# A fused hybrid decoder layer on one core: x turned unscaled as it lands, the first norm's factor spread over partitions by a product with ones

## The reference, cut to what matters

```python
xn = x * rsqrt(mean(x * x, axis=-1) + 1e-6) * g_mix      # 256 tokens, 2048 features
proj = xn @ w_in                                          # w_in: 2048 x 6144
xx = token_shift(xn) - xn
x_w, x_a, x_g = (xn + xx * mu_x[j] for j in range(3))     # inputs of three small products
# differential attention on the first 3072 columns of proj, RWKV-7 on the last 3072,
# output projection, second RMSNorm, top-2 of 32 SwiGLU experts, final RMSNorm
```

## Time and profile before

| what | value |
|---|---|
| median of 3 runs | 1580.76 us (1580.16 to 1580.87) |
| span of the profiled execution, first to last instruction | 1578.8 us (its own time is shown as this span alone) |
| PE busy | 1338.9 us, 85% |
| DVE busy | 454.4 us, 29% |
| ACT busy | 323.8 us, 21% |
| POOL busy | 44.0 us, 3% |
| moved by DMA | 481.06 MB, 305 GB/s on the mean |

### The profile page before, as it was taken

How to read it: one execution, slowest core, us unless ns; L and a number is a source line. 1 busy time by engine, 2 the same in 40 slices (tenths; PEclk the granted TensorE clock), 3 DMA queues, 4 the chain that set the end, 5 groups by cost and what they waited for, 6 DMA issues and landing times.

```text
span 1578.8 us, 22501 instructions
## 1 busy us (share of the span) xinstructions
PE 1338.9 (85%) x9378; PEld 722.1 (46%) x9378; DVE 454.4 (29%) x1100; ACT 323.8 (21%) x760; POOL 44.0 (3%) x95
## 2 busy tenths in 40 slices
PE   7999999999999999987776886876876877867776
PEld 6888888888886545422222222222221222222223
DVE  6032646767644641401101101101101101111103
ACT  1013112344422421211111111111111111111112
POOL 3000000001110000000000000000000000000000
PEclk9999999999999999998989888888888888897988
DMA  9433322222334267599999999999999999999996
GB/s 306 162 107 107 107 81 82 81 82 83 108 110 158 87 237 322 204 433 433 429 434 430 433 430 433 430 433 431 433 432 432 432 432 432 432 433 431 433 430 265
DMA packets 62055, 481.06 MB, mean 305 GB/s; under 512 B 8565, under 2 KB 27654, under 8 KB 48934
## 3 DMA queue, kind: packets, MB, share of 16 engines
q1 hardware_dynamic: 61106, 478.89, 74.3%
q10 hardware_dynamic: 884, 1.23, 0.2%
HBM read 478.01 MB, written 2.10 MB: 304 GB/s over the span
## 4 chain that ended last, share of the span: by engine, by line
PE 56%; DMA 41%; DVE 1%; ACT 1%; issue 1%; DVEq 0%; SPq 0%; ACTq 0%
DMA ring<-in_moe_w_gate_dram 22%; DMA ring<-in_moe_w_up_dram 17%; PE ps L960 11%; PE ps L773 9%; PE ps L1203 8%; PE ps L1045 7%; PE ps L1222 3%; PE ps L1179 3%; DMA ring<-in_moe_w_down_dram 2%; PE ps L846 2%; PE ps L989 2%; PE ps L1230 2%; PE ps L834 1%; PE ps L1214 1%; PE ps L852 0%
## 5 line engine op out<-in xcount | busy, mean ns | idle before, releaser
L1203 PE MATMUL ps<-ring,oT 128*32 128x512 f32 x2048 | 333.5, 811 | 205.3 <-DMA ring<-in_moe_w_gate_dram 115.2
L1203 PEld LDWEIGHTS ps<-ring,oT 128*32 128x32 f32 x2048 | 82.6, 142 | 452.1 <-issue 310.6
L960 PE MATMUL ps<-xT,ring 128*128 128x256 f32 x768 | 185.1, 388 | 0.0
L2136 DVE TENSOR_TENSOR oT<-oT,ps 128x128 f32<-128x128 f32 x32 | 9.2, 287 | 582.8 <-ACT oT L1587 582.8
L960 PEld LDWEIGHTS ps<-xT,ring 128*128 128x128 f32 x768 | 140.3, 190 | 20.6
L773 PE MATMUL ps<-xT,ring 128*128 128x256 f32 x640 | 139.5, 380 | 0.0
L773 PEld LDWEIGHTS ps<-xT,ring 128*128 128x128 f32 x640 | 121.2, 190 | 17.8 <-issue 1.5
L1222 PE MATMUL ps<-ring,oT 128*32 128x512 f32 x1024 | 117.9, 600 | 8.7 <-DVE oT L2136 7.8
L1179 PE MATMUL ps<-xT,oT 128*32 128x512 f32 x512 | 115.3, 1030 | 0.4 <-DVE oT L2124 0.4
L1045 PE MATMUL ps<-ring,oT 128*128 128x512 f32 x256 | 113.3, 594 | 0.8 <-ACT oT L1539 0.8
L1214 PEld LDWEIGHTS ps<-fold,oT 128*128 128x128 f32 x512 | 59.6, 192 | 39.7 <-issue 39.7
(11 more groups left out here) (336 smaller groups left out, 1247.1 us busy)
## 6 DMA issues: line engine op xcount, KB each, us to landing
ring<-in_moe_w_gate_dram SPq DMA_DIRECT2D x32, 4096.0 KB, 32.5
ring<-in_moe_w_up_dram SPq DMA_DIRECT2D x31, 4096.0 KB, 33.2
ring<-in_moe_w_down_dram SPq DMA_DIRECT2D x31, 4096.0 KB, 32.5
ring<-in_w_in_dram SPq DMA_DIRECT2D x24, 1024.0 KB, 5.2
ring<-in_w_in_dram SPq DMA_DIRECT2D x32, 768.0 KB, 4.8
ring<-in_w_out_dram SPq DMA_DIRECT2D x16, 1024.0 KB, 5.5
ring<-in_moe_w_up_dram SPq DMA_DIRECT2D x2, 2048.0 KB, 10.9
ring<-in_moe_w_down_dram SPq DMA_DIRECT2D x2, 2048.0 KB, 30.8
```

Of the source, the lines that this page charges most:

```text
L960: last = mm(ps[:, 6 + (par + c) % 2, 0:S], wv[:, k, c * P:(c + 1) * P], xT[:, kq * KQ + k, :], start=(kq == 0 and k == 0), stop=(kq == 3 a ...
L1203: last = mm(ps[c * B:(c + 1) * B, 1 + j, :], xe[:, par, k, :], w[:, k, :], start=(kq == 0), stop=(kq == 3), tile_position=(0, c * B))
```

## The change

The tile `xn` goes. PE turns x itself, each token half as soon as it has landed (`s_x`). The factor takes another way: DVE multiplies the identity by it (`scales`, a diagonal matrix of 128 tokens for each token half); PE multiplies a matrix of ones by that, which puts the factor of token j into column j of every partition; DVE copies these 256 columns out of the right half of PSUM's bank 7 (`spread`). `xT` is then made by one operation a block, turned block x g_mix (per partition) x `spread` (per column), and DVE does all 16 (before, DVE and ACT did 8 each). The copy of the turned rows to `vec` goes from DVE to ACT, ahead of its four lambda loads. Blocks 14 and 15 are turned after `spread` has been copied (`s_vec` 2), since block 15 goes to where the product lay. Two small operations of DVE (`omka`, `subg`) move behind the 16. ACT's semaphore `s_xTa` goes; PE waits for `s_xT` with doubled counts.

```diff
--- before.py
+++ after.py
@@ -260,7 +260,6 @@
         s_xn = sem("xn_ready")
         s_xt = sem("xn_turned")
         s_xT = sem("xT_ready")
-        s_xTa = sem("xT_ready_by_scalar")
         s_pr = sem("rkv_block_projected")
         s_prA = sem("rkv_block_copied")
         s_mix = sem("lora_input_mixed")
@@ -479,7 +478,8 @@
         SOLVES = ((0, 1), (2,), (3, 4), (5, 6), (7,), (8,), (9,), (10,), (11,))
         DENSE = (4, 2, 2, 3, 2, 3, 2, 3, 3)
         HALVES = (4, 6, 7, 9, 10, 12, 13, 14)
-        xn = oT.rearrange("p k s -> p (k s)").rearrange("p (t d) -> p t d", t=TT)
+        scales = oT[:, 0, :].rearrange("p (t q) -> p t q", t=TT)
+        spread = oT[:, 1, :]
 
         def load_rows(eng, dst, group):
 
@@ -722,23 +722,26 @@
 
             def turn(k, t):
                 return pe.transpose(ps[:, k // 2, (k % 2) * S + t * P:(k % 2) * S + (t + 1) * P],
-                                    xn[:, t, k * P:(k + 1) * P], ident[:, :])
-
+                                    res[:, t, k * P:(k + 1) * P], ident[:, :])
+
+            pe.wait_ge(s_x[0], 16)
             for k in range(KT - 2):
-                if k % 8 == 0:
-                    pe.wait_ge(s_xn, k // 8 + 1)
                 turn(k, 0)
             pe.wait_ge(s_rows, 16 * ROW_LOADS)
             pe.transpose(vec_ps[:, 0:NA_ROWS], rows_a[0:NA_ROWS, :], ident[0:NA_ROWS, 0:NA_ROWS])
             pe.transpose(vec_ps[:, NA_ROWS:NA_ROWS + NB_ROWS], rows_b[0:NB_ROWS, :],
                          ident[0:NB_ROWS, 0:NB_ROWS]).then_inc(s_vecT, 1)
+            pe.wait_ge(s_x[1], 16)
             for k in range(KT - 2):
-                if k % 8 == 0:
-                    pe.wait_ge(s_xn, k // 8 + 3)
                 last = turn(k, 1)
                 if k % 2:
                     last.then_inc(s_xt, 1)
             pe.wait_ge(s_vec, 1)
+            for t in range(TT):
+                pe.wait_ge(s_xn, t + 1)
+                last = mm(ps[:, 7, S + t * P:S + (t + 1) * P], ones[:, :], scales[:, t, :], start=True, stop=True)
+            last.then_inc(s_vecT, 1)
+            pe.wait_ge(s_vec, 2)
             for k in (KT - 2, KT - 1):
                 for t in range(TT):
                     last = turn(k, t)
@@ -756,17 +759,14 @@
 
             def rkv_block(n, fold=False, outs=False):
                 for kq in range(4):
-                    pe.wait_ge(s_xT, 2 * kq + 2)
-                    pe.wait_ge(s_xTa, 2 * kq + 2)
+                    pe.wait_ge(s_xT, 4 * kq + 4)
                     pe.wait_ge(s_ring[kq], n * 16 + 16)
                     wv = eslot[kq].rearrange("p (k n) -> p k n", k=KQ)
                     for c in range(4):
                         if kq == 0:
                             pe.wait_ge(s_prA, n * 4 + c + 1)
-                        if kq == 0 and c == 2:
-                            pe.wait_ge(s_xT, 4)
-                        if kq == 0 and c == 3:
-                            pe.wait_ge(s_xTa, 4)
+                        if kq == 0 and c >= 2:
+                            pe.wait_ge(s_xT, 2 * c + 2)
                         if kq == 0 and outs:
                             pe.wait_ge(s_l3, 2 * MT + MT // 2 + c + 1)
                         for k in range(KQ):
@@ -1324,17 +1324,14 @@
                 act.wait_ge(s_hsq, t + 1)
                 a.activation(rs[:, t:t + 1], ss[:, t:t + 1], ACT.Sqrt, bias=ssv[:, TT + t:TT + t + 1],
                              scale=1.0 / D).then_inc(s_std, 1)
+            act.wait_ge(s_vecT, 1)
+            a.copy(vec[:, 0:NA_ROWS + NB_ROWS], vec_ps).then_inc(s_vec, 1)
             act.dma_start(lamrow[:, 0, :], da_lambda_q1.broadcast_to([P, 64])).then_inc(s_lam, 16)
             act.dma_start(lamrow[:, 1, :], da_lambda_k1.broadcast_to([P, 64])).then_inc(s_lam, 16)
             act.dma_start(lamrow[:, 2, :], da_lambda_q2.broadcast_to([P, 64])).then_inc(s_lam, 16)
             act.dma_start(lamrow[:, 3, :], da_lambda_k2.broadcast_to([P, 64])).then_inc(s_lam, 16)
 
             act.wait_ge(s_vec, 1)
-            for b in (1, 3, 5, 7):
-                act.wait_ge(s_xt, b + 1)
-                for k in (2 * b, 2 * b + 1):
-                    a.activation(xT[:, k, :], ps[:, b, (k % 2) * S:(k % 2 + 1) * S], ACT.Copy,
-                                 scale=col(V_GMIX + k)).then_inc(s_xTa, 1)
             def rkv_copies(n):
                 for c in range(4):
                     if c < 3:
@@ -1653,23 +1650,23 @@
                 v.tensor_scalar(ssv[:, TT + t:TT + t + 1], ssv[:, t:t + 1], 1.0 / D, 1e-6, ALU.mult, ALU.add).then_inc(s_hsq, 1)
                 dve.wait_ge(s_std, t + 1)
                 own.mark(v.reciprocal(rs2[:, t:t + 1], rs[:, t:t + 1]))
-                own.join()
-                for half in (slice(0, D // 2), slice(D // 2, D)):
-                    v.tensor_scalar(xn[:, t, half], res[:, t, half], rs2[:, t:t + 1], None, ALU.mult).then_inc(s_xn, 1)
-            dve.wait_ge(s_vecT, 1)
-            v.tensor_copy(vec[:, 0:NA_ROWS + NB_ROWS], vec_ps).then_inc(s_vec, 1)
-            dve.wait_ge(s_vec, 1)
+                if t == 0:
+                    dve.wait_ge(s_mask, 3)
+                own.join()
+                v.tensor_scalar(scales[:, t, :], ident[:, :], rs2[:, t:t + 1], None, ALU.mult).then_inc(s_xn, 1)
+            dve.wait_ge(s_vecT, 2)
+            v.tensor_copy(spread, ps[:, 7, S:2 * S]).then_inc(s_vec, 1)
+            dve.wait_ge(s_vec, 2)
+            for k in range(KT):
+                if k % 2 == 0:
+                    dve.wait_ge(s_xt, k // 2 + 1)
+                v.scalar_tensor_tensor(xT[:, k, :], ps[:, k // 2, (k % 2) * S:(k % 2 + 1) * S], col(V_GMIX + k), spread,
+                                       ALU.mult, ALU.mult).then_inc(s_xT, 1)
+
             dve.wait_ge(s_mask, 4)
             own.mark(v.tensor_scalar(omka, col(V_KA, MT), -1.0, 1.0, ALU.mult, ALU.add))
             own.mark(v.tensor_scalar(subg, col(V_SUB), 1.0 - LAM0, None, ALU.mult))
-            for b in (0, 2, 4, 6):
-                dve.wait_ge(s_xt, b + 1)
-                for k in (2 * b, 2 * b + 1):
-                    v.tensor_scalar(xT[:, k, :], ps[:, b, (k % 2) * S:(k % 2 + 1) * S], col(V_GMIX + k), None,
-                                    ALU.mult).then_inc(s_xT, 1)
-
-            dve.wait_ge(s_xT, 8)
-            dve.wait_ge(s_xTa, 8)
+            dve.wait_ge(s_xT, KT)
             own.mark(v.tensor_tensor(diff[:, :, 1:S], xT[:, :, 0:S - 1], xT[:, :, 1:S], ALU.subtract))
             own.mark(v.tensor_scalar(diff[:, :, 0:1], xT[:, :, 0:1], -1.0, None, ALU.mult))
             own.join()
```

## The result

The changed kernel takes 1583.18 us (median of 20 runs, 1580.50 to 1585.03), the kernel before 1580.64 us beside it (20 runs, 1579.69 to 1581.67). The ratio is 1.0014, 95% interval [1.0008, 1.0021], so the change costs 1.3 to 3.3 us. That is within 0.2% by its middle, and a loss. The scatter has grown too, from 2.0 to 4.5 us.

The account below looks back on a forecast made before the run. PE was taken as the bound, with nothing covering the head before the first projection matmul. Rows, second turns, product, copy and VectorE's blocks moved its start from 15.62 to 17.03: 1580.76 + 1.4 = 1582.2 us, range 1579.7 to 1584.8.

Parts of the forecast that it names:

- The whole effect is the shift of the first projection matmul: Head: nothing covers what precedes this matmul, so its start's move from 15.62 to 17.03, +1.4 us, passes to the end.
- the sign that the whole is wrong: At the end: the end moves by another amount than the first projection matmul does.
- The 3.0 us do not arrive: Head: PE's first turns start 3.0 us earlier, at 6.36, but PE then waits for vector rows landing at 10.3.
- The second turns run at the lower level: PE's 14 turns of x's second half go at TensorE's lower clock: 2.98 us, from 11.0 to 13.98.
- this rival: Second turns: the clock rises early, they cost 1.53 instead of 2.98, start 15.6, total 1580.8 us; chance 0.28.
- The product at 0.44: Behind the second turns: two products, two records each at 0.109 with the clock up, 0.44 us, to 14.42.
- Copy and VectorE's chain: Ahead of the projection: copy 0.42 plus 0.05 wait, four block operations 1.68, then 0.15 to PE, ending at 17.03.
- PE's share: Whole kernel: PE 56%, busy nine tenths or more from the second slice on through the first half.
- The cover: VectorE's 16 blocks end 4.5 us later and the mixes near 39; PE wants them at 71.04: 32 us of cover.
- The clock falls in the new gap, 1583.9: Ahead of the projection: block 0's matmuls start at half speed, 1.7 us more; fallen clock or late rows together 0.11.
- late rows: Rows landing after 10.3, each us adding one, 1585.8 us at 12.2; with the fallen clock, chance 0.11.
- The total, 1582.2: Whole kernel: 1580.76 + 1.4 = 1582.2 us; forecast chance 0.50.

Follow-up runs that it names:

- both kernels that put the rows elsewhere: Changed kernel with PE turning the rows after the second half's blocks (1580.76 us), or with SP's row loads issued between x's halves (1580.84 us).
- the kernel that starts after two blocks: Changed kernel with the first projection matmuls waiting for two of VectorE's 16 blocks instead of four; median 1581.33 us, ratio 1.0004 to the kernel before.
- the filled kernel: Changed kernel with six turns of x's first half repeated while PE would wait for the rows; median 1581.13 us, ratio 1.0005 to the kernel before.
- the rows behind: Changed kernel with PE turning the rows after the second half's blocks instead of before them; median 1580.76 us, ratio 1.0004.
- both gaps filled: Changed kernel with six first-half turns repeated ahead of the rows and blocks 14 and 15 turned four times; median 1580.92 us, ratio 1.0004.
- warmed kernel before: Kernel before, with 21 turns of the identity on PE ahead of x's first scaled half; median 1581.08 us against 1580.65, ratio 1.0002.

## Why the prediction was right, and where it was short

- *The whole effect is the shift of the first projection matmul.* Right: 2.15 us of shift in the trace, 2.2 us by the ratio of the runs. The profiled span moved by 2.9, 0.75 more than the start, which I had named as the sign that the whole is wrong; 0.47 of that appears in the router's stage, where the clock fell at another moment, and no experiment was made on it.
- *The 3.0 us do not arrive, because PE then waits for the rows.* Right: PE stood 0.93 us for them, and the wait was gone in both kernels that put the rows elsewhere. They let PE go at 10.64 (10.4 in the prediction), and in the kernel before PE's first turns had covered them.
- *The second turns run at the lower level.* Right in both executions of the changed kernel (3.04 us against 2.98), but not a constant of it: with the same list up to there, the kernel that starts after two blocks shows the early rise. I gave this rival 0.28.
- *The product at 0.44.* **This is the term that was mis-sized.** Its records took 0.85, since I let the clock rise just ahead of it, at the time of the kernel before. Even that time was misread: from 12.93, seven turns 0.213 apart end at 14.4, where the eleven fast ones of the earlier trace rows begin, so the rise was at 14.3 to 14.4 and not at 14.1, and my product (13.98 to 14.42) lay ahead of it. Of the 0.74 us between the forecast start (17.03) and the measured one (17.77), which is also past my 16.8 to 17.3, the product up to VectorE's copy is 0.34 (1.09 against 0.75: 0.41 more in the records, 0.07 less behind them), the later rows with their slower turn 0.27, VectorE's chain 0.08 and the turns 0.06.
- *Copy and VectorE's chain.* 0.46 to the next operation against 0.47; 0.39 a block against 0.40; 1.91 from the first operation to PE against 1.83. Right, and the operation with its second tensor costs the same as the one without.
- *PE's share.* PE is at nine tenths in slices 2 to 17 of the 40, not through the whole first half as I read the earlier trace rows; nothing hangs on it.
- *The cover.* The mixes end at 39.6 (33.15 + 6.41) against "near 39", and PE did not wait for one.
- *The clock falls in the new gap, 1583.9.* Happened in one of two executions, at 1584.03. The fall itself cost the 1.7 us of the sum; that the total fits as well is in part luck, since the start there was 0.6 later than forecast. I gave it 0.11 together with late rows, and how often it happens is not shown by two executions.
- *The total, 1582.2.* The median, 1583.18, stands 1.0 above it. The later start explains 0.74 of that by itself, so the range held although the shift of 1.4 was half of that too small.
- By the Trainium skill (TensorE: Matmul & The Clock Gate, "What's actually happening") the same kernel may meet the clock's steps at different moments. The traces agree: the changed kernel's second turns took 3.25 us in two executions and 1.75 in the kernel that starts after two blocks, whose list is the same up to them; and behind like pauses the clock fell in one of the two executions and not in the other.

## What to carry to other kernels

When a wait is taken away from the front of an in-order list, look for the next wait in that list that the first one had covered, and reorder around it before counting a gain. On TensorE a pause early in the kernel can cost more than its own length: with six useless turns in a gap of 0.93 us the median was 2 us lower here, most of what the change had cost. And where it is left to chance when the clock steps, the median can hide several modes, so one trace is not enough: here the first trace of the filled kernel alone would have credited the filling with a rise that came ahead of it.

## What the runs showed of the hardware that I had not expected

- The column of the granted clock said 1.00 while turns still ran at half pace (421 ns and 0.213 us apart, before the first rise); the spacing of equal instructions is the surer sign. Later falls do appear in it, as 0.50 above.
- Read from the spacing of PE's records, the clock rose 2.7 to 5.0 us after PE's first work in all seven traced executions in which PE had no pause ahead of the rise (from 9.35 to 14.3 in the kernel before, from 6.49 to 9.3 with the rows behind, from 6.45 to 11.4 with both gaps filled). In the four with a pause of 0.6 to 0.9 us ahead of the rows it rose once by 10.37, at most 4.0 us after the first work, and three times only 7.5 to 9.4 us after it. That is a tendency of eleven executions, not a rule.
- The clock fell about 0.9 us after PE had resumed full work, behind three microseconds of which PE had worked 0.48, 0.40 and 0.38 (15 to 18 us in the second execution of the changed kernel); behind 0.48, 0.54 and 0.23 in the first it stayed up.
- VectorE's operation on two float32 tensors, one in PSUM, goes at 0.39 us for 256 columns from start to start, the same as with one tensor from PSUM and a number (both 6.36 us for 16).
- Whether the 0.65 us of earlier start in the warmed kernel before reach its end stays open: the interval of its runs is wider than that.
